# Setup of a two-layer token mixer: modulation weights in four blocks of their own, first groups fed two feature tiles at a time, and two reordered stage ends

## The chip, the cores and the metric

The kernel runs on one core of one Trainium2 chip. The metric is the device time of one execution in microseconds (us), lower is better; the runs given are the median of three. The trace is one profiled execution of the same program.

## The reference, cut to what matters

Two layers of a conditioned mixer (`x` of 512 tokens, `ctx` of 256 tokens, 1024 features), then one block of another kind (not touched here). Per layer:

```python
sh1, sc1, g1, sh2, sc2, g2 = split(silu(c) @ w_mod[l] + b_mod[l], 6)        # and the same for c_ctx
u  = x * (1 + sc1) + sh1;   uc = ctx * (1 + csc1) + csh1
y, yc = token_mixer(u, uc, ...)     # u @ w_in -> convolution, mLSTM and latent attention; gated merge @ w_out
x  = layer_norm(ALPHA * x + g1 * y, ln1_g, ln1_b)
h  = square(relu((x * (1 + sc2) + sh2) @ w1 + b1)) @ w2 + b2
x  = layer_norm(ALPHA * x + g2 * h, ln2_g, ln2_b)
```

Everything is fp32. Products are made from a high and a low part of each operand: high x high, high x low, low x high, so each 128-column group of weights costs three matmuls per feature tile and token range.

## The kernel before, in words

**Weights.** All big weights go through a ring of `SLOTS = 4` slots (`core.ring`), 128 columns x 1024 rows (512 KB) a slot, loaded by SyncE (SP) in the order of `plan_weights`, each when `weights_used` says that its slot is free. A group of weights is then split: ScalarE (ACT) rounds it into one of two high slots (`high_part`, L365), GpSimd (POOL) subtracts (`low_part`, L374). `product` (L448, matmuls at L470, L471, L475) needs the high part from the start and the low part for its last third. `paired_products` (L493, matmuls at L505, L506, L510) runs the first two groups of a stage interleaved, feature tile k by feature tile k, so that features may arrive while it runs. Both take `between` hooks.

**Setup (`setup_stage`).** The first 16 groups of `w_mod` of layer 0 (shift 1 and scale 1, 8 MB) are the first run `mod0` of the ring. SP issues the constants, four ring groups, `x`, `ctx`, then the other twelve groups as slots come free, then the first four groups of `w_in`. TensorE (PE) turns each pair of groups into rows of sums (`mod_rows_pair`, L723), with the transposes of the tokens in between (L681), copied to `core.x` by VectorE (DVE, L702); then it transposes nine tiles of small vectors (L688, each waits for a copy at L705), turns the rows back to columns (`turn_mod_rows`, L732), and DVE adds the bias and the one (`mod_finish`, L740, L745). Only then `Modulated.make_high` (ACT, L830, L836) and `make_low` (DVE, L848, L863) make the features of layer 0 tile by tile, and the first product of the projection starts (`project_stage`, PE L505).

**Attention end (`attention_stage`).** Head pairs p are worked through in steps i over key tiles. The sums of pair p-1 are inverted by DVE during pair p (`invert`, L1846) at the steps of `inverse_at`; POOL then divides (L1777), and `invert_last` (L1856) of the last pair waits for that division, because both use the same tile. Behind it on DVE stands a copy of modulation rows (`copy_mods`, L1866) on which PE's last `turn_mod_rows` (L732) waits.

**MLP head (`out_mlp_stage`, once per layer).** After `w_out` the first layer norm's sums are taken by PE in the middle of the first paired products of `w1` (after tile `SUMS_AFTER` = 4). ACT takes the logarithm and the exponential, DVE refines the root in three instructions (L3282, L3284), and only then evicts group 0: `cols` (L3292, L3293), `pre` from PSUM (L3298), which frees the PSUM tile for the next product. In the same loop DVE normalises the residual (L3304, L3306) and ACT scales it (L3178). In layer 0 tiles are 768 tokens wide, in layer 1 512.

```python
for q in range(KT):
    dve.wait_ge(used.sem, group_done(core, run, i, q))
    ...
    ins = nc.vector.scalar_tensor_tensor(piece(pre), piece(mean), cols[:, j:j + 1], result[j](q % 2), ALU.mult, ALU.add)
    ins.then_inc(free[q % 2].sem, 1)
```

## Time and profile before

| | us |
|---|---|
| median of 3 runs (lowest, highest) | 3375.93 (3370.58, 3377.02) |
| the profiled execution | 3375.39 |
| its span | 3373.6 |
| mean granted TensorE clock | 0.983 |

| engine | busy us | share |
|---|---|---|
| PE (matmul) | 3247.3 | 96% |
| PE weight load | 2600.0 | 77% |
| DVE | 1870.1 | 55% |
| ACT | 1180.1 | 35% |
| POOL | 1093.2 | 32% |

An engine's busy time is the time in which it executes instructions; the waits of an engine are listed with the instruction that released it. "Granted clock" is TensorE's clock as a share of full speed: 1.00 is 2.4 GHz, 0.50 is 1.2 GHz.

### The profile page before, as it was taken

Reading aid. Unit: us, or ns where it says so; the run is one execution under the profiler, and the core shown is the slowest. Engines: PE = TensorE matmul, PEld = TensorE weight load, DVE = VectorE, ACT = ScalarE, POOL = GpSimd, SP = SyncE. Lnnn points to the kernel's source line nnn. Section 1 sums busy time; section 2 is a strip of 40 time slices with the busy share of each in tenths; the row PEclk is TensorE's granted clock in tenths of the full one; section 3 lists DMA queues with packets and bytes.
Section 4 is the critical chain, followed back from the end, with each engine's and each line's share of the span. In section 5 each row is a group of like instructions: output and inputs, shape, how many; then the busy total and the mean of one; then the engine's idle time right before and its main releaser. Section 6 shows DMA issues by size and latency. Waiting matters only on the chain. (4 is left out here: it accounts for less than half of the span.)

```text
span 3373.6 us, 48742 instructions
## 1 busy us (share of the span) xinstructions
PE 3247.3 (96%) x18116; PEld 2600.0 (77%) x18116; DVE 1870.1 (55%) x2848; ACT 1180.1 (35%) x1670; POOL 1093.2 (32%) x551
## 2 busy tenths in 40 slices
PE   5999999999999999999999999999999989999998
PEld 4888655788888888888776457778888867788886
DVE  2869466622368242245997564138333575777634
ACT  2233333631244132233542436234322364323223
POOL 2433100422233322222441014443444424344442
PEclk8999999999999999999999999999999989999999
DMA  6222255022221222222322341332333321233332
GB/s 187 63 61 55 49 155 152 17 60 63 63 63 57 63 63 63 63 63 62 88 75 47 107 119 45 93 94 81 94 93 93 91 74 51 82 93 93 95 96 78
DMA packets 549133, 270.17 MB, mean 80 GB/s; under 512 B 55922, under 2 KB 547146, under 8 KB 548827
## 3 DMA queue, kind: packets, MB, share of 16 engines
q1 hardware_dynamic: 547330, 267.20, 28.0%
q8 instruction: 127, 2.08, 0.3%
q14 instruction: 51, 0.42, 0.0%
q10 hardware_dynamic: 889, 0.30, 0.0%
q0 software_dynamic: 736, 0.17, 0.0%
HBM read 265.50 MB, written 2.10 MB: 79 GB/s over the span
## 5 line engine op out<-in xcount | busy, mean ns | idle before, releaser
L374 POOL TENSOR_TENSOR weights_low<-weight_ring,weights_high 128x1024 fp32r<-128x1024 f32 (+1 forms) x403 | 965.4, 2397 | 1755.3 <-ACT weights_high L365 1754.9
L365 ACT ACTIVATE weights_high<-weight_ring 128x1024 fp32r<-128x1024 f32 (+1 forms) x408 | 410.0, 1005 | 1132.3 <-PE ps L475 1048.7
L470 PE MATMUL ps<-features_high,weights_high 128*128 128x512 f32 (+1 forms) x1888 | 640.1, 354 | 4.7 <-DVE features_low L2476 4.6
L471 PE MATMUL ps<-features_low,weights_high 128*128 128x512 f32 (+1 forms) x1888 | 636.4, 353 | 0.0
L470 PEld LDWEIGHTS ps<-features_high,weights_high 128*128 128x128 f32 x1888 | 356.0, 189 | 64.7 <-DVE features_low L2476 6.5
L471 PEld LDWEIGHTS ps<-features_low,weights_high 128*128 128x128 f32 x1888 | 355.6, 188 | 55.1 <-issue 0.2
L475 PE MATMUL ps<-features_high,weights_low 128*128 128x512 f32 (+1 forms) x1888 | 383.8, 351 | 0.0
L470 PE MATMUL ps<-u_high,weights_high 128*128 128x512 f32 (+2 forms) x944 | 369.3, 394 | 11.5 <-ACT weights_high L365 3.3
L471 PE MATMUL ps<-u_low,weights_high 128*128 128x512 f32 (+2 forms) x944 | 362.8, 388 | 0.0
L475 PEld LDWEIGHTS ps<-features_high,weights_low 128*128 128x128 f32 x1888 | 304.6, 188 | 47.0
L1249 DVE SCALAR_TENSOR_TENSOR conv<-conv,vectors 128x512 f32<-128x512 f32 (+1 forms) x480 | 306.3, 707 | 1.2 <-DVE conv L1157 0.9
L470 PE MATMUL ps<-mlp_u_high,weights_high 128*128 128x512 f32 (+1 forms) x960 | 273.3, 314 | 7.6 <-DVE arena L3298 7.6
L471 PE MATMUL ps<-mlp_u_low,weights_high 128*128 128x512 f32 (+1 forms) x960 | 271.0, 313 | 0.0
L3235 DVE SCALAR_TENSOR_TENSOR x_features<-ps,modulation,x_features 128x512 f32<-128x512 f32 x118 | 74.8, 661 | 314.5 <-PE ps L475 302.9
L475 PE MATMUL ps<-u_high,weights_low 128*128 128x512 f32 (+2 forms) x944 | 227.5, 384 | 0.0
L470 PEld LDWEIGHTS ps<-u_high,weights_high 128*128 128x128 f32 (+1 forms) x944 | 180.2, 191 | 59.0 <-issue 9.6
L2498 DVE TENSOR_TENSOR arena<-ps,arena 128x768 f32<-128x768 f32 (+3 forms) x48 | 39.5, 823 | 329.9 <-PE ps L475 329.6
L471 PEld LDWEIGHTS ps<-u_low,weights_high 128*128 128x128 f32 (+1 forms) x944 | 179.8, 190 | 39.0 <-issue 1.2
L475 PEld LDWEIGHTS ps<-u_high,weights_low 128*128 128x128 f32 (+1 forms) x944 | 170.8, 187 | 38.1 <-issue 0.5
L470 PEld LDWEIGHTS ps<-mlp_u_high,weights_high 128*128 128x128 f32 x960 | 184.0, 192 | 20.8 <-issue 8.1
L471 PEld LDWEIGHTS ps<-mlp_u_low,weights_high 128*128 128x128 f32 x960 | 183.8, 191 | 11.0
L3169 ACT ACTIVATE arena<-arena,seam 128x512 f32<-128x512 f32 x96 | 59.1, 647 | 291.2 <-DVE arena L3301 291.2
(609 smaller groups left out, 4927.5 us busy)
## 6 DMA issues: line engine op xcount, KB each, us to landing
weight_ring<-in_w_in SPq DMA_DIRECT2D x262, 256.0 KB, 3.2
weight_ring<-in_w SPq DMA_DIRECT2D x256, 256.0 KB, 3.0
weight_ring<-in_w_mod SPq DMA_DIRECT2D x192, 256.0 KB, 3.7
weight_ring<-in_w_up SPq DMA_DIRECT2D x88, 256.0 KB, 3.1
weight_ring<-in_w_out SPq DMA_DIRECT2D x48, 256.0 KB, 3.3
weight_ring<-in_w_down SPq DMA_DIRECT2D x32, 256.0 KB, 3.2
weight_ring<-in_w_mla_out SPq DMA_DIRECT2D x32, 128.0 KB, 2.3
weight_ring<-in_w_conv_out SPq DMA_DIRECT2D x32, 128.0 KB, 2.3
```

Source lines behind the costliest of these rows:

```text
L365: act.activation(core.ring_high[:, split_slot(run, q), 0:n], core.ring[:, slot, 0:n], ACT.Copy).then_inc(core.high_ready.sem, 1)
L374: pool.tensor_tensor(core.ring_low[:, split_slot(run, q), 0:n], core.ring[:, (run.first + q) % SLOTS, 0:n], high.bitcast(F32), ALU.subtrac ...
L470: pe.matmul(to, w_high[:, k, 0:m], high(k, a, b), start=(first and k == ks[0]), stop=False, skip_group_check=True)
L471: pe.matmul(to, w_high[:, k, 0:m], low(k, a, b), start=False, stop=False, skip_group_check=True)
L475: mm = pe.matmul(out[:, at:at + b - a], w_low[:, k, 0:m], high(k, a, b), start=False, stop=(last and k == ks[-1]), skip_group_check=True)
L1249: nc.vector.scalar_tensor_tensor(conv[:, f, a:b], pads[:, f, bass.ds(t + at, b - a)], w_dw[:, bass.ds(t, 1), f], conv[:, f, a:b], ALU.mult ...
L2498: nc.vector.tensor_tensor(dst, gemm(core, 2 + f, w), sig[:, f, 0:w], ALU.mult).then_inc(multiplied.sem, 1)
L3169: ins = act.activation(tmp[:, a:b], pre[:, a:b], ACT.Relu, bias=cols[:, ns + j:ns + j + 1])
L3235: ins = nc.vector.scalar_tensor_tensor(x, gemm(core, q % 2)[:, a:b], mod[:, gates + q, j:j + 1], x, ALU.mult, ALU.add)
```

## The change

Four edits. In the setup, the 16 modulation groups leave the ring: `FirstModulation` holds them in four blocks (m = 0 to 3) of 2 MB, two of them in a new allocation `near` and two in the arena, each with shift and scale of feature tiles 2m and 2m+1. SP issues the constants, the tokens in three loads, block 0, two ring groups of `w_in`, the last 18 small vector loads (taken from ACT's queue), blocks 1 to 3, two more ring groups. Only block 0 is turned before the projection; the others are turned by hooks inside the first paired products, and ACT and DVE make the features two tiles at a time. The tokens are transposed one tile of 128 tokens after the other, and the vectors' nine transposes have a PSUM place each and are copied by two instructions. In the projection SP waits until two ring groups are used before it loads `rope` (whose place `near` had) and goes on with the ring.

```diff
-            add(f"mod{l}", MOD_FIRST, plain(w_mod), split=False)
...
+    def make_rows(self, pe, m):
+        pe.wait_ge(self.loaded[m].sem, self.loaded[m].at(32))
+        for kind in range(2):
+            w, to = self.blocks[m][:, :, kind, :], self.in_rows[kind]
+            for half in range(KT // 2):
+                for j in range(COND_TILES):
+                    k, g = 2 * half + j % 2, j // 2
+                    mm = pe.matmul(to[j * COND_ROWS:(j + 1) * COND_ROWS], self.core.cond[:, k, :], w[:, k, g * P:(g + 1) * P],
...
+            mm.then_inc(self.made.sem, 1)
+    def copy_rows(self, act, m):
+        for kind in range(2):
+            act.wait_ge(self.made.sem, self.made.at(2 * m + kind + 1))
+            act.activation(self.rows[:, 2 * m + kind], self.in_rows[kind], ACT.Copy).then_inc(self.copied.sem, 1)
+    def turn_rows(self, pe, m):
+        for n in range(2 * m, 2 * m + 2):
+            pe.wait_ge(self.copied.sem, self.copied.at(n + 1))
+            mm = pe.matmul(self.sums[:, 4 * n:4 * n + 4], self.rows[:, n], self.core.cond_pick, start=True, stop=True)
+        mm.then_inc(self.turned.sem, 1)
+    def finish(self, dve, m):
...
+            if kind:
+                ins = v.scalar_tensor_tensor(mod[:, at:at + 2, :], sums, 1.0, bias, ALU.add, ALU.add)
+            else:
+                ins = v.tensor_tensor(mod[:, at:at + 2, :], sums, bias, ALU.add)
...
     def _(sp):
         sp.dma_start(core.base, a["base"]).then_inc(base_in.sem, 16)
+        for n in range(0, NT, 2):
+            sp.dma_start(tokens[:, n:n + 2], source.rearrange("(n p) c -> p n c", p=P)).then_inc(tokens_in[n // 2].sem, 16)
+        first.load(sp, 0)
+        load_weights(core, sp, LEAD)
+        load_vectors(sp, ACT_SHARE, len(tiles), sp_loaded)
+        for m in range(1, 4):
+            first.load(sp, m)
         load_weights(core, sp, SLOTS)
...
+        sp.wait_ge(used.sem, core.runs[f"conv{l}"].first + (2 if seam is None else 0))
         sp.dma_start(core.rope, core.rope_input).then_inc(core.rope_loaded.sem, 16)
...
+        first_mods = {0: lambda: core.first.make_rows(pe, 1), 1: lambda: turn_and_make(1, 2), 2: lambda: core.first.turn_rows(pe, 2),
+                      3: lambda: core.first.make_rows(pe, 3), 4: lambda: core.first.turn_rows(pe, 3)}
...
@@ project_stage, scalar (ACT) @@
+            for m in range(4):
+                core.u.make_high(act, range(2 * m, 2 * m + 2), lambda k: core.first.wait(act, k // 2))
+                if m < 3:
+                    core.first.copy_rows(act, m + 1)
@@ project_stage, vector (DVE) @@
+            for m in range(4):
+                if m:
+                    core.first.finish(dve, m)
+                core.first.wait(dve, m)
+                core.u.make_low(dve, range(2 * m, 2 * m + 2))
```

In the attention, the inversions during the last pair move to its first steps:

```diff
     inverse_at = {0: [(0, 0)], 2: [(0, 1)], 4: [(1, 0)]} if both else {0: [(0, 0)], 5: [(0, 1)]}
+    inverse_at_last = {0: [(0, 0)], 1: [(0, 1)], 2: [(1, 0)]} if both else {0: [(0, 0)], 1: [(0, 1)]}
...
+            for ctx, which in (inverse_at if p + 1 < PAIRS else inverse_at_last).get(i, []) if p else []:
+                invert(p - 1, ctx, which)
```

In the MLP head, DVE evicts the first two groups before it refines the root (the second into a tile and columns of its own), ACT splits the next two groups of weights between logarithm and exponential and behind it, the residual is normalised in the second half of the first quarter, the sums are taken one tile later in layer 1, and ACT splits the last early group before the squares of a tile:

```diff
+SUMS_AFTER = (4, 5)
@@ scalar (ACT) @@
         for k in range(KT):
             g = k + LEAD
             if g < KT:
                 high_part(core, act, run_out, g // 4, g % 4)
             else:
                 high_part(core, act, run, 0, g - KT)
+            if k == KT - 1:
+                square(made(KT - 2))
...
         act.activation(rstd[:, 0:w], var[:, 0:w], ACT.Ln, bias=core.eps[:, 0:1]).then_inc(s["logged"].sem, 1)
+        ahead(core, act, run, 0, 0, False)
...
+        ahead(core, act, run, 0, 1, False)
...
+                if first_here and q >= 2:
                     ahead(core, act, run, i, q, last)
@@ vector (DVE) @@
+        for q in range(2):
+            evict(0, q)
         step = s["rstd_step"]
...
+                if not (isinstance(i, int) and i == 0 and q < 2):
+                    evict(i, q)
...
-                    nc.vector.tensor_tensor(x, x, mean[:, 0:w], ALU.subtract).then_inc(s["centered"].sem, 1)
-                    nc.vector.tensor_tensor(x, x, rstd[:, 0:w], ALU.mult).then_inc(s["normalised"].sem, 1)
...
+                if first_here:
+                    for n in (0, 1) if q == 0 else range(q + 1, min(q + 2, KT)):
+                        normalise(n)
```

The order of SP's queue in the setup, before:

```order
L645 DMA constants<-in_base 128x900
L308 DMA weight_ring<-in_w_mod 128x4x128 x8
L647 DMA arena<-in_x 128x4x1024
L648 DMA arena<-in_ctx 128x2x1024
...
L308 ISA [waits weights_used_0]
L308 DMA weight_ring<-in_w_mod 128x4x128
```

and with the change:

```order
L717 DMA constants<-in_base 128x900
L720 DMA features<-in_x 128x2x1024 x2
L720 DMA features<-in_ctx 128x2x1024
L608 DMA first_modulation<-in_w_mod 128x8x256 x2
L305 DMA weight_ring<-in_w_in 128x4x128 x4
L695 DMA arena<-in_ffn_conv_w 22x128 [waits rows_cleared_21]
...
L700 DMA arena<-in_c_norm_g 1x64 x2
L608 DMA first_modulation<-in_w_mod 128x8x256 x2
L608 DMA arena<-in_w_mod 128x8x256 x4
L305 DMA weight_ring<-in_w_in 128x4x128 x4
L1030 DMA rope<-in_rope 128x1152 [waits weights_used_0]
```

The tokens stand ahead of all modulation weights, three quarters of these stand behind two ring groups and the small vectors, and no load of the setup waits for a slot any more.

PE from the setup into the first paired products, with the change (before, the eight L732 matmuls all stand ahead of the first L505; L502, L503, L507 are the lines that were L505, L506, L510):

```order
L751 MATMUL ps<-constants,features 128x128 x48
L618 MATMUL ps<-first_modulation,conditions 32x128 x32
L761 MATMUL ps<-constants,arena 128x128 x9
L632 MATMUL ps<-constants,arena 128x4 x2
...
L502 MATMUL ps<-features_high,weights_high 128x256
L503 MATMUL ps<-features_low,weights_high 128x256
L618 MATMUL ps<-first_modulation,conditions 32x128 x32
L502 MATMUL ps<-features_high,weights_high 128x512
...
L632 MATMUL ps<-constants,arena 128x4 x2
L618 MATMUL ps<-arena,conditions 32x128 x32
```

Three of four blocks of the modulation are now made (L618) and turned (L632) between feature tiles of the first pair.

DVE in the MLP head of layer 1, before:

```order
L3277 TENSOR_SCALAR arena<-arena 128x512 [waits at_conv_step_82]
L3282 TENSOR_TENSOR arena<-arena 128x512 [waits at_conv_squared_80,at_conv_step_82]
L3282 TENSOR_TENSOR arena<-arena 128x512 [waits at_conv_squared_80]
L3284 SCALAR_TENSOR_TENSOR arena<-arena 128x512 [waits at_conv_squared_80]
L3292 TENSOR_SCALAR seam1<-ps 128x1 [waits weights_used_0,at_conv_scaled_83,at_conv_squared_80]
L3293 TENSOR_SCALAR seam1<-ps,vectors 128x1
L3298 SCALAR_TENSOR_TENSOR arena<-arena,seam1,ps 128x512 [waits at_conv_centered_79]
L3301 TENSOR_TENSOR arena<-arena 128x512 [waits product_tile0_free_3]
L3304 TENSOR_TENSOR x_features<-x_features,arena 128x512
```

and with the change (L3398 was L3298, L3406 and L3408 were L3282 and L3284, L3422 was L3301):

```order
L3383 TENSOR_SCALAR arena<-arena 128x512 [waits at_conv_step_94]
L3392 TENSOR_SCALAR seam1<-ps 128x1 [waits weights_used_0,at_conv_scaled_95,at_conv_step_94]
L3393 TENSOR_SCALAR seam1<-ps,vectors 128x1
L3398 SCALAR_TENSOR_TENSOR arena<-arena,seam1,ps 128x512 [waits at_conv_centered_91]
L3392 TENSOR_SCALAR seam1<-ps 128x1 [waits weights_used_0]
L3393 TENSOR_SCALAR seam1<-ps,vectors 128x1
L3398 SCALAR_TENSOR_TENSOR arena<-arena,seam1,ps 128x512 [waits at_conv_centered_91]
L3406 TENSOR_TENSOR arena<-arena 128x512 [waits at_conv_squared_92] x2
L3408 SCALAR_TENSOR_TENSOR arena<-arena 128x512 [waits at_conv_squared_92]
L3422 TENSOR_TENSOR arena<-arena 128x512 [waits product_tile0_free_3,at_conv_squared_92]
```

The two evictions stand ahead of the three instructions of the refinement, and L3304, L3306 are no longer among the evictions. (Semaphores carry the name of their first use.)

## Rows read from the trace of the kernel before

**Rows 1.** The page, busy time of each engine, share of the span, instructions.

```profile
PE 3247.3 (96%) x18116; PEld 2600.0 (77%) x18116; DVE 1870.1 (55%) x2848; ACT 1180.1 (35%) x1670; POOL 1093.2 (32%) x551
```

**Rows 2.** Waits of PE, whole span (total us, times, longest us).

```profile
PE ps L723 <- DMA weight_ring<-in_w_mod: 16.3, 6, 3.8
...
PE ps L505 <- DVE features_low L863: 12.3, 4, 4.7
...
PE ps L470 <- DVE arena L3298: 7.6, 2, 4.1
```

**Rows 3.** Timeline of the setup: SP's queue and PE (start us, us, what).

```profile
0.75 0.40 SPq L645 DMA_DIRECT2D constants<-in_base  x1
...
1.20 6.12 SPq L308 DMA_DIRECT2D weight_ring<-in_w_mod  x8
...
8.58 0.85 SPq L648 DMA_DIRECT2D arena<-in_ctx  x1
...
23.66 2.82 PE L681 MATMUL ps<-constants,arena 128*128 128x128 f32 x12 [7.14 <-DMA arena<-in_ctx]
...
28.37 1.08 PE L723 MATMUL ps<-weight_ring,conditions 128*32 128x128 f32 x32 [1.89 <-DMA weight_ring<-in_w_mod]
```

**Rows 4.** DMA issues, 0 to 60 us (KB each, median us to landing).

```profile
constants<-in_base SPq DMA_DIRECT2D x1, 450.0 KB, 3.7
```

**Rows 5.** Two setup stretches: length, PE, PEld, DVE, ACT, POOL busy; PEclk, DMA, GB/s.

```profile
15.00:20.00 5.00, 1.52 (x31) 1.06 (x20) 0.00 (x0) 0.00 (x0) 0.00 (x0) 1.00 1.05 371
...
40.00:45.00 5.00, 4.74 (x67) 3.74 (x56) 1.91 (x2) 0.00 (x0) 0.00 (x0) 0.66 0.98 284
```

**Rows 6.** Timeline, end of the setup and first paired products.

```profile
54.32 0.69 PE L688 MATMUL ps<-constants,arena 128*128 128x128 f32 x2 [0.17 <-DVE vectors L705]
...
61.61 0.17 DVE L745 TENSOR_SCALAR modulation<-modulation 128x16 f32<-128x16 f32 x1
...
64.48 0.76 PE L505 MATMUL ps<-features_high,weights_high 128*128 128x512 f32 x1 [3.14 <-DVE features_low L863]
...
79.91 2.94 PE L510 MATMUL ps<-features_high,weights_low 128*128 128x512 f32 x16
...
82.93 0.47 PE L470 MATMUL ps<-features_high,weights_high 128*128 128x512 f32 x1
```

**Rows 7.** Timeline, MLP head of layer 0, PE and DVE.

```profile
1045.24 2.98 PE L510 MATMUL ps<-mlp_u_high,weights_low 128*128 128x512 f32 x16
...
1051.71 0.77 PE L470 MATMUL ps<-mlp_u_high,weights_high 128*128 128x512 f32 x1 [3.49 <-DVE arena L3298]
...
1050.42 1.14 DVE L3298 SCALAR_TENSOR_TENSOR arena<-arena,seam,ps 128x512 f32<-128x512 f32 x2
```

**Rows 8.** Timeline, MLP head of layer 1, PE, DVE and POOL.

```profile
2321.86 0.38 PE L505 MATMUL ps<-mlp_u_high,weights_high 128*128 128x256 f32 x1 [2.42 <-ACT weights_high L365]
...
2338.64 0.55 PE L470 MATMUL ps<-mlp_u_high,weights_high 128*128 128x256 f32 x1 [4.09 <-DVE arena L3298]
...
2346.83 0.28 PE L470 MATMUL ps<-mlp_u_high,weights_high 128*128 128x256 f32 x1
...
2334.68 2.71 DVE L3284 SCALAR_TENSOR_TENSOR arena<-arena 128x512 f32<-128x512 f32 x1
...
2334.43 2.41 POOL L374 TENSOR_TENSOR weights_low<-weight_ring,weights_high 128x1024 fp32r<-128x1024 f32 x1 [9.99 <-ACT weights_high L365]
```

**Rows 9.** Stretches at either clock level, columns as in rows 5.

```profile
1051.00:1054.00 3.00, 2.29 (x7) 1.94 (x8) 2.93 (x5) 1.38 (x3) 0.00 (x0) 0.50 0.12 35
...
1057.00:1060.00 3.00, 3.00 (x18) 2.65 (x18) 2.97 (x4) 0.00 (x0) 2.21 (x1) 0.96 0.00 0
...
2347.00:2350.00 3.00, 3.00 (x27) 3.00 (x27) 2.90 (x7) 0.80 (x2) 0.00 (x0) 1.00 0.55 162
```

**Rows 10.** Timeline, attention end of layer 1, DVE and PE.

```profile
2000.65 1.76 DVE L1856 RECIPROCAL conv<-ps 128x256 f32<-128x256 f32 x1 [1.45 <-POOL features L1777]
...
2002.61 0.49 PE L732 MATMUL ps<-constants,conv 128*128 128x4 f32 x2 [2.38 <-DVE conv L1866]
```

More of the change, by code:

```diff
@@ L658, in _ @@
         act.activation(core.cond[:, :, 0:2], cond_turn.rearrange("p (j k) -> p k j", k=KT), ACT.Silu).then_inc(cond_ready.sem, 1)
-        load_vectors(act, SHARE, len(tiles), loaded)
-        act.wait_ge(core.weights_used.sem, run.first + run.groups)
-        act.activation(mod_rows[:, half:], in_rows[:, half:], ACT.Copy).then_inc(rows_copied.sem, 1)
+        load_vectors(act, POOL_SHARE, ACT_SHARE, act_loaded)
+        first.copy_rows(act, 0)
         first_high_parts(core, act, core.runs["conv0"])
@@ L683, in _ @@
-        pe.wait_ge(pool_loaded.sem, 16 * n_vec(0, SHARE))
-        pe.wait_ge(loaded.sem, 16 * n_vec(SHARE, len(tiles)))
+        for n in range(NT):
+            pe.wait_ge(tokens_in[n // 2].sem, 16)
+            if n >= 2:
+                pe.wait_ge(token_copied.sem, 2 * (n - 1))
+            for f in range(KT):
+                mm = pe.transpose(turn_of(n)[:, f * P:(f + 1) * P], tokens[:, n, f * P:(f + 1) * P], core.ident)
+            mm.then_inc(turned.sem, 1)
+        pe.wait_ge(cond_ready.sem, 1)
@@ L690, in _ @@
-        pe.wait_ge(turn_free.sem, 2 + KT + len(tiles))
-        pe.wait_ge(rows_copied.sem, 2)
-        turn_mod_rows(core, pe, lambda pair: mod_rows[:, pair * P:(pair + 1) * P], MOD_FIRST // 2, sums).then_inc(rows_turned.sem, 1)
+            mm = pe.transpose(vector_turn(n), rows[:, n, :], core.ident)
+        mm.then_inc(vectors_turned.sem, 1)
+        first.turn_rows(pe, 0)
     @block.vector
     def _(dve):
-        dve.sem_inc(turn_free.sem, 2)
-        for f in range(4):
+        for f in range(2, 4):
@@ L699, in _ @@
             dve.sem_inc(core.tile_free[f].sem, 1)
-        for f in range(KT):
-            dve.wait_ge(turned.sem, f + 1)
-            nc.vector.tensor_copy(core.x[:, f, :], psum(f)).then_inc(turn_free.sem, 1)
-        for n in range(len(tiles)):
-            dve.wait_ge(turned.sem, KT + n + 1)
-            nc.vector.tensor_copy(core.vec[:, n * P:(n + 1) * P], psum(n)[:, 0:P]).then_inc(turn_free.sem, 1)
-        dve.wait_ge(core.weights_used.sem, run.first + run.groups)
-        nc.vector.tensor_copy(mod_rows[:, 0:half], in_rows[:, 0:half]).then_inc(rows_copied.sem, 1)
@@ L1278, in project_stage @@
         core.u.passed()
+        core.first.passed()
     else:
@@ L3007 @@
 SEAM = 64
-SUMS_AFTER = 4
+SUMS_AFTER = (4, 5)
 def out_mlp_stage(core, l, seam):
```

213 lines of the change are left out of this document (131 added, 82 removed).

## The prediction

> **What bounds the kernel now.** I read the page first. TensorE is busy for 96% of the span and no other engine for more than 55% [rows 1], so time is to be had only where PE stands still or runs at the lower clock level. The second view is therefore PE's own waits [rows 2]. They show three things that the change touches: 16.3 us for modulation weights in the setup, 12.3 us for the low parts of features, and 7.6 us in two waits for an eviction, one at each MLP head. A fourth, 2.38 us, is at the attention end of layer 1 [rows 10]. The third is the timeline at each place. In the setup SP issues constants and eight ring loads before the tokens, and PE gets the last of these, `ctx`, at 23.66 [rows 3]. All bytes issued up to it are 450 + 8 x 256 + 2048 + 1024 = 5570 KB, or 5.70 MB, and they took 23.66 - 0.75 = 22.9 us: 249 GB/s. The DMA engines are full both in a stretch with the tokens (371 GB/s) and in one with ring loads alone (284 GB/s) [rows 5]. Twelve further groups of modulation weights follow through the ring, the vectors are still being turned at 54.32, and the first product of the projection starts at 64.48, ends its pair at about 82.9 [rows 6]. What counts is when that pair ends: from there PE is never short of work for long.
>
> The sum is made against the profiled execution, 3375.39 us, which is 0.5 us below the median of 3375.93. About 0.2% (7 us) is what a measurement of this kernel can tell from no change.
>
> **The setup, step by step.** *Start of the first product.* SP now issues constants, tokens, block 0 and two groups of `w_in` (the two DMA groups together 3.15 MB), in all 450 + 3072 + 2048 + 1024 = 6594 KB, or 6.75 MB, and then 18 small loads of vectors; the nine transposes of the vectors need all of it. At the 249 GB/s of before it has landed at 0.75 + 27.1 = 27.9; at 284 to 371 GB/s at 19 to 24.5. The early stretch starts slowly, but the block's rows are 1 KB long where the ring's are 512 bytes, so I take 26. Then nine transposes at 0.69 / 2 us [rows 6] are 3.1 us, two copies of 1152 columns together 1.7 (768 took 1.14 [rows 7]), two matmuls and two DVE instructions (0.17 each [rows 6]) for block 0 0.5, and from ready modulation to first product 64.48 - 61.78 = 2.7 us as before [rows 6]. 26 + 3.1 + 1.7 + 0.5 + 2.7 = 34.0, with 28 and 37 as ends.
>
> *The pair.* Its eight feature tiles took 79.91 - 64.48 = 15.4 us, 1.93 each, and the 16 low products that end it 3.0 [rows 6]. To them come three times 32 small matmuls (1.08 us where they ran fastest [rows 3]) and three times two turning ones (0.4): 4.5 us. From each turning PE cannot go on to the next two feature tiles until DVE has finished the block (0.4) and the features are made (2.7): 3.1 us, in part under the matmuls of the next block or of the second tile. I get about 2.0, 1.7 and 1.4 us of standing still for the blocks 1, 2 and 3. The last block is landed 6.29 MB after 26, at 43 to 51; PE asks for it at about 47. So the pair ends at 34.0 + 15.4 + 4.5 + 5.1 + 3.0 = 62.0. These gaps pull the clock down at times: the same 3 us held 7 matmuls in 2.29 us at 0.50 and 27 at 1.00 in another stage [rows 9]; I add 2. **64 instead of 82.9, 19 us less.** The ends are 69.5 (249 GB/s throughout, lower level) and 59.
>
> On the queues: POOL's four vector tiles instead of three and ACT's three are issued while the tokens move; on SP the wait for two used groups holds back `rope` and ring group 4, and behind them every later weight. It ends with the pair, and two further groups, already in the ring, give PE 16 us (48 matmuls each at 6 per us [rows 9]) for one `rope` and one group, some 1.1 MB: hidden. DVE's and ACT's later work in the stage moves with PE.
>
> *Where a rule of the notes applies.* The clock was 0.66 from 40 to 45 us, in a setup full of breaks [rows 5], and 0.50 after a wait of 3.49 us [rows 7, 9]: PE's breaks decide the level. The Trainium skill, "TensorE: Matmul & The Clock Gate", Part 1 (the HAM clock gate), says that "the default state is throttled, and activity releases the throttle", which speaks against cutting the first pair into pieces with waits between them. By it the whole pair would run at the lower level, which is a rival below; the trace agrees with it at the places named and says nothing on breaks as short as those expected here.
>
> **MLP head, layer 0.** The pair ends at 1048.2, the next product starts at 1051.71 because its tile is freed by DVE's eviction at 1050.42 [rows 7]. With the eviction ahead of the refinement, DVE has group 0 out while the second group's 16 low products run, and the high part needed is split earlier too. The 3.5 us go. The lower level that follows lasts until about 1057 (0.96 is the mean from there on [rows 9]), 5.3 us at 7 / 2.29 = 3.1 matmuls per us against 18 / 3 = 6: 2.6 us, which go with the wait. 6 us. Behind it, DVE refines and handles groups 0 and 1 and reaches the eviction of group 2 at about 1065, when PE needs that tile (two groups of 48 matmuls after 1048.2, at 6 per us): nothing to spare, so the lower end is 3.
>
> **MLP head, layer 1.** PE first waits 2.42 us for ACT's high part, which stands behind two squares [rows 8]; it now stands ahead of one of them: 2.1 us less. The wait of 4.09 us for the eviction goes. The group that follows ran from 2338.64 to 2346.83 [rows 8], 8.2 us, at the lower level, against 48 x 3.00 / 27 = 5.3 at the upper [rows 9]: 2.7. That is 8.9. What is late next: DVE evicts group 2 only behind the refinement and the finishing of groups 0 and 1, at about 2344.2, 0.5 later than PE wants it, and POOL's subtraction may stretch one instruction of it, as L3284 took 2.71 us beside a POOL instruction of 2.41 us [rows 8]. I take 1.4 for both: **7.5**, ends 5 and 9. The Trainium skill, "SBUF — State Buffer", "SBUF: two separate sides", has the port pair of DVE and GpSimd as an exclusive lock, in which the loser waits for the whole instruction; by it the stretch falls onto whichever DVE instruction POOL meets, and the trace agrees with 2.71 us. The residual's normalising, two DVE instructions and one or two of ACT per tile, moves into the second half, where DVE has one addition per product: hidden.
>
> **Attention ends.** In layer 1 DVE waits 1.45 us for POOL's division before its last inversions, and PE then 2.38 us for a copy behind them [rows 10]. With the inversion done five steps earlier the division is long over: 1.6 us less, up to 4 if the lower level that follows goes too, 0 at least. In layer 0 no such wait is seen: 0.
>
> **Sum.** 19 + 6 + 7.5 + 1.6 = 34.1; 3375.4 - 34.1 = 3341.3, and 0.5 for the median: **3342 us**.
>
> **Rivals.**
> - *The lower level through the whole pair.* Breaks of 1 to 2 us between short bursts hold PE at 0.50. For: 0.50 to 0.66 in the setup [rows 5]. Against: after the wait of 2.42 us [rows 8] PE went on at the upper level. The pair's 18.4 + 4.5 us become up to 1.9 times as long, of which the waits take back 5, and 2 were already counted: about 10 us more, 3352.
> - *The heads give it back.* DVE is late for group 2 in both layers, because the refinement now comes behind two evictions and under a POOL subtraction: 2 and 3 us stay of 6 and 7.5. 3342 + 8.5 = 3350.
> - *The blocks land together.* Everything is in the queue within some 20 us; if the loads share the engines rather than follow each other, block 0 and the vectors land late, at about 35, and the pair ends at 72: 3350. For: the 249 GB/s up to 23.66 us is less than either stretch shows, as if later loads had taken a part. Against: `ctx`, the last of eleven loads, still came at 23.66 [rows 3].
> - *Better than that.* 340 GB/s, no lower level in the pair, clean heads, the clock at the attention end: 23 + 7 + 9 + 3.5 = 42.5, 3333.
> - *Slower than before.* The 18 small loads on SP's queue take their turn one behind the other. At the 3.7 us from issue to landing of the constants [rows 4], with 18 in a row, the vectors would be complete at 26 + 67 = 93, and the pair would end near 131: 48 us later than before, 15 given back elsewhere, 3409. It decides from 34 / 18 = 1.9 us each. Against: eight ring loads and two large ones, issued by 9.4, had all landed by 23.66 [rows 3], so loads of one queue run beside each other.
> - *It does nothing where it says.* If DMA bandwidth alone sets the pair's end, 13.2 MB at 249 GB/s is 53.8, and it cannot come before 60: still 3342. There is no room for no change at all in the setup.
>
> **How the numbers follow.** Forecast 0.50; lower level 0.17; heads 0.12; blocks together 0.07; better 0.10; slower 0.02; the rest, a mishap that eats all but the bound, 0.02. The forecast's own range is 3336 to 3348. The range to hold 8 in 10 takes in most of the two rivals above and the better case: 3333 to 3356. All but the last two are faster by over 0.2%: 0.96; within 0.2% 0.02, slower 0.02.
>
> **What would show it.** Right: first product of the projection at 31 to 37 us and the next product after the pair at 60 to 68; DVE's evictions ahead of the refinement with PE going from the pair into group 2 with no wait in either layer; no wait over 1 us before group 4; POOL's division before the last inversions. Wrong: the vectors' transposes later than 30, PE waits for w_mod of over 3 us inside the pair, a granted clock near 0.5 from 34 to 60, or a new wait of PE for L3398 at group 4.

## The result, and the profile after

The median of the changed kernel is 3346.81 us (3343.38 to 3351.27, 5 runs) against 3375.93 (3370.58 to 3377.59, 5 runs): a ratio of 0.9917, 95% interval 0.9905 to 0.9928, or 29.1 us less. 34 were forecast. A second measurement of the same kernel (`changed_again`, below) gave 23.9 us less. The profiled execution took 3347.69 us, 27.7 less than the one before; the ledger below is made against that.

The page, its head, the busy line and the line of the clock:

```profile
span 3345.8 us, 48674 instructions
...
PE 3238.5 (97%) x18116; PEld 2594.1 (78%) x18116; DVE 1905.9 (57%) x2850; ACT 1183.5 (35%) x1677; POOL 1092.4 (33%) x552
...
PEclk8999999999999999999999999999999999999999
```

PE is busy for 8.8 us less than in [rows 1], though it has the same products to make. The mean granted clock rose from 0.983 to 0.986, which by proportion (an estimate) is some 10 us of 3247, so the lower busy time fits the clock; the rest of the gain is waits. PE's waits, longest in total first (engine, line waited for, us in total, times, longest):

```profile
PE ps L502 <- DVE features_low L939: 16.1, 6, 4.7
...
PE ps L618 <- DMA first_modulation<-in_w_mod: 4.5, 1, 4.5
PE ps L467 <- DVE features_low L3427: 3.7, 2, 3.4
```

Of the waits of [rows 2], 16.3 us for modulation weights (L723) became 4.5 (L618), and the 7.6 for evictions are gone but for 0.9. The wait for low parts of features (L505, now L502) rose from 12.3 to 16.1, and one is new: 3.7 us, of which 3.4 in one piece, for `hidden_low` (L3427).

SP's queue in the setup (start, time to issue), for [rows 3]:

```profile
2.69 6.89 SPq L608 DMA_DIRECT2D first_modulation<-in_w_mod  x2
9.62 10.34 SPq L305 DMA_DIRECT2D weight_ring<-in_w_in  x4
20.00 1.94 SPq L695 DMA_DIRECT2D arena<-in_ffn_conv_w  x3
...
26.95 1.02 SPq L608 DMA_DIRECT2D first_modulation<-in_w_mod  x2
```

From 20.00 to 26.91 SP issued the small loads. They are 19, three of `ffn_conv_w` and sixteen behind them, where the texts on record count 18.

PE in the setup and the pair, for [rows 3] and [rows 6]:

```profile
21.36 3.64 PE L618 MATMUL ps<-first_modulation,conditions 128*32 128x128 f32 x64 [4.46 <-DMA first_modulation<-in_w_mod]
28.20 2.15 PE L761 MATMUL ps<-constants,arena 128*128 128x128 f32 x9 [3.20 <-DMA arena<-in_c_norm_g]
...
35.07 0.76 PE L502 MATMUL ps<-features_high,weights_high 128*128 128x512 f32 x1 [4.06 <-DVE features_low L939]
...
38.53 3.04 PE L618 MATMUL ps<-first_modulation,conditions 128*32 128x128 f32 x64
...
43.79 1.96 PE L618 MATMUL ps<-arena,conditions 128*32 128x128 f32 x64
46.59 0.50 PE L502 MATMUL ps<-features_high,weights_high 128*128 128x512 f32 x1 [0.84 <-DVE features_low L939]
...
58.96 0.50 PE L502 MATMUL ps<-features_high,weights_high 128*128 128x512 f32 x1 [2.01 <-DVE features_low L939]
...
62.56 2.94 PE L507 MATMUL ps<-features_high,weights_low 128*128 128x512 f32 x16
65.59 0.47 PE L467 MATMUL ps<-features_high,weights_high 128*128 128x512 f32 x1
```

The vectors were complete at 28.20, the first product started at 35.07, and the next product after the pair at 65.59 where it was 82.93 [rows 6].

Layer 0's head, for [rows 7]: from the pair into group 2 without a wait.

```profile
1025.81 2.98 PE L507 MATMUL ps<-mlp_u_high,weights_low 128*128 128x512 f32 x16
1028.62 0.39 PE L467 MATMUL ps<-mlp_u_high,weights_high 128*128 128x512 f32 x1
```

Layer 1's head, PE, for [rows 8]: the product of group 2 at 2303.39 needs no wait, group 4 waits 0.86 us, and the end of w2's first product 3.41.

```profile
2290.88 0.36 PE L502 MATMUL ps<-mlp_u_high,weights_high 128*128 128x256 f32 x1 [1.55 <-DVE x_features L3341]
...
2303.39 0.28 PE L467 MATMUL ps<-mlp_u_high,weights_high 128*128 128x256 f32 x1
...
2315.77 0.36 PE L467 MATMUL ps<-mlp_u_high,weights_high 128*128 128x256 f32 x1 [0.86 <-DVE arena L3398]
...
2347.07 0.50 PE L467 MATMUL ps<-features_high,weights_high 128*128 128x512 f32 x1 [3.41 <-DVE features_low L3427]
```

The same place, DVE's work for group 2 and POOL's subtraction beside it:

```profile
2306.11 2.77 DVE L3408 SCALAR_TENSOR_TENSOR arena<-arena 128x512 f32<-128x512 f32 x1
...
2314.88 0.75 DVE L3398 SCALAR_TENSOR_TENSOR arena<-arena,seam,ps 128x512 f32<-128x512 f32 x1
2315.66 2.15 DVE L3422 TENSOR_TENSOR arena<-arena 128x512 f32<-128x512 f32 x1
2318.60 0.69 DVE L3424 TENSOR_TENSOR arena<-arena 128x512 f32<-128x512 f32 x1 [0.79 <-ACT arena L3277]
2319.34 0.69 DVE L3427 TENSOR_TENSOR features_low<-arena,features_high 128x512 fp32r<-128x512 f32 x1
```

```profile
2305.59 2.74 POOL L371 TENSOR_TENSOR weights_low<-weight_ring,weights_high 128x1024 fp32r<-128x1024 f32 x1 [0.78 <-ACT weights_high L362]
2314.88 2.38 POOL L371 TENSOR_TENSOR weights_low<-weight_ring,weights_high 128x1024 fp32r<-128x1024 f32 x1 [6.56 <-ACT weights_high L362]
```

L3398, with an operand in PSUM, takes 0.75 us beside POOL's L371. L3422, a multiply of two tiles in SBUF that takes 0.69 alone (the first one at 2308.91 does), takes 2.15. It is so in each of the six groups 2 to 7. The attention end of layer 1, for [rows 10]:

```profile
1974.39 0.39 PE L808 MATMUL ps<-constants,conv 128*128 128x4 f32 x2 [0.68 <-DVE conv L1955]
1974.71 1.08 PE L799 MATMUL ps<-weight_ring,conditions 128*32 128x128 f32 x32
```

**The ledger.** The start of the same PE instruction in both traces, the earlier start in the changed kernel being the gain so far: after the pair 17.3 us; before layer 0's head 19.4; behind it 25.1; ahead of the attention end of layer 1 26.5 and behind it 30.1; in layer 1's head 31.0 at the first wait, 35.3 at group 2, 37.8 at group 3, 36.8 at group 4, 36.7 at the start of w2 and 31.4 at its second product; at the end 27.8. So the setup gave 17.3, layer 0's head 5.7, the attention end 3.6, and layer 1's head 1.3: it gained 6.6 and gave 5.3 back. Stretches of unchanged work between them added 2.1 and 1.4 us and took 3.6 in the last block.

### The profile page after: what moved, and what is told of

Its sections match the earlier page's. It is cut to its first block and busy times, and to the rows that moved or that the text cites. A ratio compares the mean times of both kernels' runs of the same rounds, so it can differ in the third digit from the quotient of the medians.

```text
span 3345.8 us, 48674 instructions
## 1 busy us (share of the span) xinstructions
PE 3238.5 (97%) x18116; PEld 2594.1 (78%) x18116; DVE 1905.9 (57%) x2850; ACT 1183.5 (35%) x1677; POOL 1092.4 (33%) x552
## 5 line engine op out<-in xcount | busy, mean ns | idle before, releaser
L371 POOL TENSOR_TENSOR weights_low<-weight_ring,weights_high 128x1024 fp32r<-128x1024 f32 (+1 forms) x403 | 963.7, 2393 | 1732.3 <-ACT weights_high L362 1732.1
L3341 DVE SCALAR_TENSOR_TENSOR x_features<-ps,modulation,x_features 128x512 f32<-128x512 f32 x118 | 74.9, 662 | 266.7 <-PE ps L472 255.1
```

The costliest lines, as they stand in the source:

```text
L371: pool.tensor_tensor(core.ring_low[:, split_slot(run, q), 0:n], core.ring[:, (run.first + q) % SLOTS, 0:n], high.bitcast(F32), ALU.subtrac ...
L3341: ins = nc.vector.scalar_tensor_tensor(x, gemm(core, q % 2)[:, a:b], mod[:, gates + q, j:j + 1], x, ALU.mult, ALU.add)
```

## The experiments

Lines are named in the text as in the changed kernel; in the rows of a run they are its own. Where the whole times are too coarse, a stretch of the trace decides. "The head's stretch" is that from the norm sums of layer 1's head to the sums at the layer's end: 2327.22 to 2696.44 in the kernel before, 369.2 us, and 2297.38 to 2665.00 in the changed one, 367.6. The changed kernel takes the sums one feature tile later, so these two do not hold the same work: counted from the same matmul, it has 368.8 against 369.2. Among the kernels with the later sums the stretch is the same work, but it varies by itself: `setup_better` and `head_only`, whose head is that of the changed kernel, have 368.8 us where that has 367.6, because the lower clock level behind the wait of 3.4 us lasted longer. A difference of under 1.2 us in it tells nothing.

### The three parts alone

`setup_only` is the kernel before with the setup's part of the diff, of which one line stands for all:

```diff
-        if l == 0:
-            add(f"mod{l}", MOD_FIRST, plain(w_mod), split=False)
```

> The kernel before with the edit of the setup alone. If the parts of the change add up, the next product after the first pair starts at 65.6 us as in the changed kernel (82.9 before), and the whole gain is 17 to 19 us: 3357 to 3359 us. The rival is that the setup's gain is coupled to the rest through clock and phase, so that alone it gives less than 15 or more than 21 us.

3357.67 us against 3376.22, ratio 0.9943 (0.9927 to 0.996): 18.6 us less, and the low products that end the pair start at 62.30, as in the changed kernel (62.56).

`head_only`, the MLP head's part:

```diff
-SUMS_AFTER = 4
+SUMS_AFTER = (4, 5)
...
+        for q in range(2):
+            evict(0, q)
         step = s["rstd_step"]
```

> The kernel before with the edits of the MLP head alone. In the changed kernel's trace layer 0 gained 5.7 us and layer 1 gained 6.6 us up to the first product of w2 and lost 5.2 us again behind it. If this giving back belongs to the head itself, it is here too: a wait of PE of about 3.4 us for hidden_low in layer 1, and 3368 to 3370 us in all. If it came from phases that the other edits shift, that wait is absent and the time is 3363 to 3365 us.

3368.45 us, ratio 0.9974 (0.9964 to 0.9984): 7.8 less. The give-back belongs to the head itself:

```profile
2341.32 0.36 PE L470 MATMUL ps<-mlp_u_high,weights_high 128*128 128x256 f32 x1 [0.86 <-DVE arena L3310]
...
2372.60 0.80 PE L470 MATMUL ps<-features_high,weights_high 128*128 128x512 f32 x1 [3.39 <-DVE features_low L3339]
```

`attention_only`:

```diff
+    inverse_at_last = {0: [(0, 0)], 1: [(0, 1)], 2: [(1, 0)]} if both else {0: [(0, 0)], 1: [(0, 1)]}
...
-            if p and i in inverse_at:
-                for ctx, which in inverse_at[i]:
-                    invert(p - 1, ctx, which)
+            for ctx, which in (inverse_at if p + 1 < PAIRS else inverse_at_last).get(i, []) if p else []:
+                invert(p - 1, ctx, which)
```

> The kernel before with the earlier inversions alone. By the prediction 1.6 us are gained at the end of attention in layer 1; by the changed kernel's trace 3.7 us, as the lower clock level behind the wait of 2.38 us goes as well. So 3372 to 3374 us, within what the measurement can tell from nothing; the place itself decides: PE's turning matmul after the second set of modulation rows no more waits 2.38 us, and the modulation matmuls behind it take 1.1 us and not 1.94.

3371.25 us, ratio 0.9985 (0.9975 to 0.9995). At the place, the wait of 2.38 us is 0.68, and the stretch around it (from the first product of keys at 1892.03 in the kernel before to the mLSTM's first eight-matmul transposes at 2020.11) takes 124.5 us instead of 128.1. `setup_only`, without the edit, has 128.1 there, but `head_only`, also without it, 126.5: up to 1.6 of the 3.6 us can be the clock. The three medians add up to 31.3 us, against 29.1 for all together: as far as medians of this spread can tell, the parts do not lean on each other.

### Why layer 1's head gave its gain back

`normalise_in_loop`: the residual's normalising in layer 1 back where it was.

```diff
                 nc.vector.tensor_tensor(made_here, made_here, rstd[:, 0:w], ALU.mult).then_inc(s["evicted"].sem, 1)
+                if not both and isinstance(i, int) and i == 0:
+                    normalise(q)
...
-                if first_here:
+                if first_here and both:
                     for n in (0, 1) if q == 0 else range(q + 1, min(q + 2, KT)):
                         normalise(n)
```

(and ACT's `residual(q)` with it).

> The changed kernel, but in layer 1 the residual is normalised inside the first quarter's loop again, as before. Theory A, POOL's subtraction stretches DVE's multiply by the root in every group (0.69 to 2.16 us), and DVE, at 5.39 us a group against PE's 5.68, never catches up: with 1.30 us more work per group, of which 0.79 fill a wait, a group costs 5.9 us, DVE falls further behind, and PE's wait for hidden_low before the end of w2's first product grows from 3.4 to some 5 to 7.5 us: 3349 to 3351 us. Theory B, moving the normalising out of the loop is what made DVE late: the wait goes, as in the kernel before, and the time is 3341 to 3343 us.

```profile
2322.21 0.36 PE L467 MATMUL ps<-mlp_u_high,weights_high 128*128 128x256 f32 x1 [1.74 <-DVE arena L3400]
...
2351.84 0.50 PE L467 MATMUL ps<-features_high,weights_high 128*128 128x512 f32 x1 [0.67 <-DVE features_low L3431]
...
2357.93 0.79 PE L467 MATMUL ps<-features_high,weights_high 128*128 128x512 f32 x1 [5.13 <-DVE features_low L3431]
```

3357.82 us, ratio 0.9947 (0.993 to 0.9964); the head's stretch took 374.1, 6.4 more than in the changed kernel. The waits grew to 0.67 and 5.13, 5.8 together, within the 5 to 7.5 of theory A; the whole missed its 3349 to 3351 by 7 us, of which 3.2 stand in the clock's stretch (42.7 us for 39.4, see `changed_again`). Theory B falls: moving the normalising out was worth 6.4 us to this order of the work.

`quarter_low`: POOL's subtraction over a quarter of the columns. Three quarters of the low parts of the weights of layer 1's MLP are left out.

```diff
-    n = run.kts[q] * P
+    n = run.kts[q] * P // (4 if run is core.runs["mlp1"] else 1)
     high = core.ring_high[:, split_slot(run, q), 0:n]
```

> The changed kernel, with POOL's subtraction for the weights of layer 1's MLP over a quarter of the columns (three quarters of those low parts are left out, so that POOL's instruction takes about 0.6 us and not 2.4). Theory A: DVE's multiply takes 0.7 us again, a group 3.9 us, DVE catches up within three groups, and PE's wait of 3.4 us for hidden_low goes with the lower clock level behind it, as does the 0.86 us wait at group 4: 3341 to 3342 us. Theory C, DVE is late because the refinement now stands behind two evictions: less than 2.1 us of the 3.4 go, 3344 to 3346 us.

DVE in groups 2 and 3 of this run:

```profile
2305.09 1.11 DVE L3408 SCALAR_TENSOR_TENSOR arena<-arena 128x512 f32<-128x512 f32 x1
...
2312.20 0.75 DVE L3398 SCALAR_TENSOR_TENSOR arena<-arena,seam,ps 128x512 f32<-128x512 f32 x1
2312.98 0.69 DVE L3422 TENSOR_TENSOR arena<-arena 128x512 f32<-128x512 f32 x1
...
2316.12 0.75 DVE L3398 SCALAR_TENSOR_TENSOR arena<-arena,seam,ps 128x512 f32<-128x512 f32 x1
2316.90 0.69 DVE L3422 TENSOR_TENSOR arena<-arena 128x512 f32<-128x512 f32 x1
```

L3422 takes 0.69 us in each group, a group 3.9 and not 5.4, the refinement (L3408) 1.11 and not 2.77. PE has no wait of over 0.6 us from group 2 to the end of w2's first product, and the head's stretch is 361.3 us, 6.3 less. The whole was 3345.3 us (ratio 0.9913, 0.9896 to 0.993), not the 3341 to 3342 of theory A and inside the 3344 to 3346 of theory C; but its four runs span 3340.8 to 3346.8, so it decides nothing. The rows decide: with POOL's instruction short both waits are gone, and nothing of the refinement's place behind two evictions is left over. Theory A stands, and theory C falls.

`last_tile_last`: w2's first two products in another order.

```diff
+                held = i == 0 and not both
+                if held:
+                    for q, ks in ((0, range(0, 7)), (1, range(0, 5)), (0, range(7, 8)), (1, range(5, 8))):
+                        product(core, pe, run, i, KT + q, use(i, KT + q), q % 2, *hidden, width=w, first=ks[0] == 0, last=ks[-1] == 7,
+                                late=1 if len(ks) == 7 else 0, ready=None if q else hidden_ready, ks=ks, done=ks[-1] == 7)
-                for q in range(KT):
+                for q in range(2 if held else 0, KT):
```

> The changed kernel, with the first two products of w2 in layer 1's first quarter taken in another order: tiles 0 to 6 for the first, 0 to 4 for the second, then tile 7 for the first and 5 to 7 for the second. Tile 7 is then wanted 3.5 us later, when it was ready. If the give-back is this wait of 3.4 us and 1.6 us of lower level behind it, 5 us go: 3341 to 3343 us. If DVE is simply behind with everything, the wait moves on to the third product, which needs its tile freed by DVE behind two normalisings: 3344 to 3346 us.

```profile
2356.30 0.50 PE L467 MATMUL ps<-features_high,weights_high 128*128 128x512 f32 x1 [1.33 <-ACT weights_high L362]
```

The wait of 3.41 is gone, and PE waits 1.33 for ACT's high part at the third product instead. The stretch is 364.2 us, 3.4 less. The whole, 3348.96 us (ratio 0.9922, 0.9905 to 0.9938), missed the 3341 to 3343 expected, and by more than those 1.3 us: other stretches were longer (see the clock, below).

### The setup

`vectors_on_act`:

```diff
-POOL_SHARE, ACT_SHARE = 4, 7
+POOL_SHARE, ACT_SHARE = 4, 9
```

> The changed kernel, with the 18 small vector loads back on ACT's queue, where loads were issued at 0.3 us each and ended at 14.6 us. SP's own issuing was held up for 10.3 us by four ring loads, so it came to the small loads at 20.0 and the vectors were complete at 28.2. Theory D, the issuing on SP bounds the vectors: they are complete at 23 to 25, the first product starts at 31 to 32 (35.07), the blocks 1 to 3 are issued 7 us earlier, and the pair ends at 59 to 62: 3341 to 3343 us. Theory E, the bytes bound them (249 GB/s up to 28.2): the vectors still come at 27 or later and the time stays at 3345 to 3348 us.

```profile
20.28 0.60 ACTq L700 DMA_DIRECT2D arena<-in_c_norm_g  x2
...
21.82 3.64 PE L618 MATMUL ps<-first_modulation,conditions 128*32 128x128 f32 x64 [5.56 <-DMA first_modulation<-in_w_mod]
25.44 1.31 PE L762 MATMUL ps<-constants,arena 128*128 128x128 f32 x9
...
33.90 0.77 PE L502 MATMUL ps<-features_high,weights_high 128*128 128x512 f32 x1 [6.81 <-DVE features_low L940]
```

The features, in the changed kernel and then in this run:

```profile
32.40 1.65 DVE L924 TENSOR_SCALAR arena<-x_features,modulation 128x512 f32<-128x512 f32 x4
```

```profile
28.80 4.09 DVE L925 TENSOR_SCALAR arena<-x_features,modulation 128x512 f32<-128x512 f32 x4
32.81 1.81 DVE L940 TENSOR_TENSOR features_low<-arena,features_high 128x768 fp32r<-128x768 f32 x2
```

```profile
26.83 4.83 POOL L371 TENSOR_TENSOR weights_low<-weight_ring,weights_high 128x1024 fp32r<-128x1024 f32 x2 [11.80 <-ACT weights_high L362]
```

The vectors no longer bound anything: their transposes follow block 0's rows at 25.44 with no wait. So it was SP's queue and not the bytes: theory E falls. But the modulation was ready 3.6 us earlier and the first product only 1.2: POOL's two subtractions, which in the changed kernel ended at 31.0, ahead of DVE's features at 32.40, now ran beside them, and L924's four instructions took 4.09 us and not 1.65. 3347.73 us, ratio 0.9917 (0.9901 to 0.9934): the expectation of 3341 to 3343 was wrong. In the setup it was so by the same mechanism as in the head, and the pair ended at 64.30, not at 59 to 62. The whole time alone lies in theory E's 3345 to 3348, but the clock's stretch (see `changed_again`) was 3.2 us longer here than in the changed kernel's trace, so the rows decide here too.

### Better versions

`setup_better` adds two edits to `vectors_on_act`, POOL's second subtraction behind the first two feature tiles and block 3's rows one hook earlier, behind feature tile 2 and not 3 (the text below says two):

```diff
-        first_low_parts(core, pool, core.runs["conv0"])
+        low_part(core, pool, core.runs["conv0"], 0, 0)
...
+        if seam is None:
+            core.u.wait(pool, 1)
+            low_part(core, pool, runs["conv"], 0, 1)
         low_parts(core, pool, runs["conv"], made=LEAD)
...
-        first_mods = {..., 2: lambda: core.first.turn_rows(pe, 2),
-                      3: lambda: core.first.make_rows(pe, 3), 4: lambda: core.first.turn_rows(pe, 3)}
+        first_mods = {..., 2: lambda: turn_and_make(2, 3),
+                      3: lambda: core.first.turn_rows(pe, 3)}
```

> The changed kernel with three edits of its setup: the small loads on ACT's queue (as in the run vectors_on_act), POOL's second subtraction of weights put behind the first two feature tiles (there the two subtractions, 4.8 us in one piece, stretched DVE's four feature instructions from 1.65 to 4.09 us), and block 3's rows made two tiles earlier. If POOL took the gain of the earlier vectors, the first product starts at 31 to 32 us (33.9 in vectors_on_act, 35.1 in the changed kernel); with rows 3 earlier PE's wait of 2.01 us before tile 6 goes too, and the next product after the pair starts at 59.5 to 61.5 (64.3 and 65.6): 3342 us, with 2 to 3 us to either side for clock phases elsewhere. If blocks 2 and 3 land too late for the faster pair, PE waits for them at the rows of block 3 and the pair ends at 62 or later.

3343.53 us, ratio 0.9904 (0.9889 to 0.9919). The first product came at 31.22, PE waited once in the pair (0.84 us), the wait of 2.01 is gone, and the next product started at 58.63 (65.59 in the changed kernel, 59.5 to 61.5 expected).

`head_better` is `last_tile_last` with ACT's `ahead` in front of two `residual` calls and with

```diff
+                early = not both and isinstance(i, int) and i == 0
+                if early and q == 1:
+                    evict(0, 2)
```

> The changed kernel with three edits of layer 1's MLP head: tile 7 wanted last (as in last_tile_last), ACT splitting the third product's weights ahead of two residual instructions (they cost PE 1.33 us there), and DVE evicting group 2 before it finishes group 1. In the place itself the waits of 0.86, 3.41 and 1.33 us are gone and the head ends 5.5 to 6 us earlier than in the changed kernel against the work ahead of it: 3341 us, again with 2 to 3 us to either side. If DVE's lag only moves on, a wait of PE for a freed tile of 1 us or more stands at w2's third or fourth product.

3348.93 us, ratio 0.9917 (0.9902 to 0.9932), and the stretch 364.9, where `last_tile_last` had 364.2: no gain, and a difference too small to call a loss. Group 2 evicted earlier moved the wait on: PE stood 0.93 us for ACT's high part at group 4 and 1.19 us for DVE at group 5. A miss.

> The six edits of setup_better and head_better together. If they add up, 10 to 11 us less than the changed kernel: 3336 us (3333 to 3340), a ratio to the kernel before of 0.988.

`both_better`: 3342.83 us (3334.69 to 3343.63), ratio 0.9895 (0.9881 to 0.9909). Slower than the 3336 expected, in part for the miss above. Without the early eviction:

> The kernel of both_better without the early eviction of group 2, which only moved the wait: there PE waited 0.93 us for ACT's high part and 1.19 us for DVE at the groups behind. The stretch from the first layer norm sums of layer 1's head to the end of that layer, 367.6 us in the changed kernel, 364.2 with tile 7 last and 364.9 in both_better, becomes 362.9 (3.4 and 1.3 us less than 367.6), the next product after the first pair starts at 59 to 60 us, and the whole is 6 + 4.7 us less than the changed kernel: 3336 us, 3333 to 3341 as the clock falls elsewhere. If ACT's order at tile 7 is worth nothing, the stretch is 364.2.

```profile
31.93 0.76 PE L502 MATMUL ps<-features_high,weights_high 128*128 128x512 f32 x1 [4.82 <-DVE features_low L940]
...
59.33 0.47 PE L467 MATMUL ps<-features_high,weights_high 128*128 128x512 f32 x1
...
2348.97 0.47 PE L467 MATMUL ps<-features_high,weights_high 128*128 128x512 f32 x1 [0.74 <-DVE x_features L3354]
```

`five_edits`: 3342.03 us (3332.62 to 3344.33), ratio 0.9899 (0.9882 to 0.9916). The pair ends 6.3 us earlier than in the changed kernel; the head's stretch is 363.7 (362.9 expected), as 0.74 us of waiting for a tile took the place of the 1.33 for the high part. Against `setup_better` (3343.53) the whole time does not tell the head's two edits from nothing; they are seen in the stretch alone.

> The changed kernel itself once more, beside five_edits on the same chip. 3346.8 us (3343 to 3351). Its stretches of identical work elsewhere tell how far the clock alone moves the time: in the traces so far the stretch from the gates' small transposes to the keys of layer 1 took 39.4 to 42.7 us, the same work in every kernel. If that is chance and no property of a program, it may be near 42 us here, where it was 39.4.

`changed_again`, the changed kernel itself, measured beside `five_edits`: 3351.60 us (3350.49 to 3351.79), ratio 0.9931 (0.9918 to 0.9945). `five_edits` is 9.6 us faster beside it, and the ranges and intervals do not meet: it beats both kernels. The clock is not the reason, as its stretch described next took 42.6 us in `five_edits` and 42.4 in `changed_again`. The changed kernel had 3346.81 in its first measurement, outside the range of the second. The clock is where the two traces part. The stretch from the gates' small transposes to the keys in layer 1, the same work everywhere, took 39.4 us there and 42.4 here; 20 us in it, windows of the changed kernel and of `changed_again` (PE, weight load, DVE, ACT, POOL busy; granted clock; DMA share; GB/s):

```profile
1760.00:1780.00 20.00, 18.44 (x118) 16.30 (x119) 19.90 (x40) 5.08 (x12) 5.11 (x2) 0.91 0.23 48
```

```profile
1760.00:1780.00 20.00, 18.03 (x100) 16.21 (x101) 19.90 (x43) 4.43 (x7) 3.24 (x2) 0.74 0.14 32
```

In the traces of this study that stretch has three values: 41.2 us in the three kernels without the edit of the MLP head (the kernel before, `setup_only`, `attention_only`), and with it 39.4 to 39.7 in four traces and 42.4 to 42.7 in seven. The changed kernel is in both of the last two groups, so no edit decides between them; what does was not tried.

## Why the prediction was right, and where not

**The setup: 19 us forecast, 17.3 measured.** The first product was due at 34.0 and came at 35.07. The step "I take 26" for the landing was wrong in kind. Block 0 had landed at 21.36 (277 GB/s for its 5.70 MB, within the bounds taken), and what came at 28.20 were the small loads, because SP got to issue them only at 20.00, after four ring loads had held it for 10.34 us. I had priced bytes and read no issue times; `vectors_on_act` shows it. Behind that the terms hold: from ready modulation to the first product 2.7 us as before, nine transposes with copies and block 0 some 4.2 where 5.3 were taken.

**The pair** was to take 28.0 + 2 and took 30.5, by luck: two errors cancel. "Three times 32 small matmuls" is the step that failed: a block is two pairs of groups, 64 matmuls in the trace (the program's 32 are recorded as two each, as the 32 of [rows 3] for one pair are), 3.0 us at the lower level and 1.96 at the upper, 7.0 in all where 3.2 were counted. Against it the gaps were 0.84 and 2.01 us, not 5.1: DVE and ACT made the features mostly under the next block's rows. The clock was 0.51 from 20 to 40 us and 0.98 from 40 to 60, so the rival of the lower level through the pair did not come. (Its own sum was off as well: 22.9 us at up to 1.9 times, less 5 and 2, are 13.6 us more and not 10.) The rule of the Trainium skill quoted for it ("TensorE: Matmul & The Clock Gate", Part 1), that throttled is the default and activity releases it, agrees with the trace as it stands: the lower level held through the first feature tile and into block 1's rows. That the whole pair would stay there did not follow: PE stood still for 0.84 and 2.01 us and went on at the upper level, 1.00 from 42 to 59 us. Nor did block 0 wait for others, nor the small loads queue one behind the other: three were issued in 0.65 us each, the others in 0.25 to 0.31.

**Layer 0's head: 6 forecast, 5.7 measured,** and steady: the stretch from its norm sums to layer 1's first waiting product is 549.9 us before and 544.2 in each of the ten traces of the changed kernel and of those built on it.

**Layer 1's head: 7.5 forecast, 1.3 measured.** The terms that were priced came: 0.9 of 2.1 for the high part (DVE's L3341 is late next there), 4.3 of 4.1 for the eviction, 2.5 of 2.7 for the level (8.2 less 5.3 is 2.9, a slip of 0.2), and 1.1 of 1.4 lost at group 4. The step that failed is "I take 1.4 for both": I followed DVE's lag to the first tile that PE wants back, and stopped. At group 2 DVE was late by one product. To catch up it needs groups shorter than PE's 5.68 us; with POOL's subtraction locked onto L3422 in every group it has 5.39, and regains 0.3 a group. So tile 7's `hidden_low` was ready at 2347.0 where PE wanted it at 2343.7, which cost 3.4 us and, at the lower level that followed, 1.7 more. `normalise_in_loop`, `quarter_low` and `last_tile_last` show the chain from both sides. The lock could have been read in the kernel before:

```profile
2342.89 2.46 DVE L3301 TENSOR_TENSOR arena<-arena 128x512 f32<-128x512 f32 x1
```

There the overlap passed: the same instruction took 0.69, 1.35, 1.13, 0.92 and 0.71 us in groups 2 to 6, as DVE kept to PE's 5.68 us a group and POOL's subtractions came every 5.46. In layer 0 L3422 is stretched too (2.92 us for 0.96), but a group of PE takes 8.5 us there and nothing waits. The rival "the heads give it back" named this cause, DVE behind under a POOL subtraction, for the wrong place and both layers. It left 5 us to the two heads, which gave 7.0, where the forecast had 13.5; its sum, 3350, lies nearer to both measurements than the forecast's 3342.

The rule of the Trainium skill on the shared port pair ("SBUF — State Buffer", "SBUF: two separate sides") says more than I used of it: it names for the lock a DVE instruction with two inputs in SBUF (against a GpSimd instruction that reads SBUF), or one in a mode that uses both ports. The rows agree: L3422 2.15 and L3408 2.77 us (0.69 and 1.11 in `quarter_low`) have two inputs in SBUF; L3398, whose second tile is in PSUM, takes 0.75 either way. L924, with one tile as input, took 4.09 us for four and not 1.65; in which mode it runs, no trace here shows.

**The attention end: 1.6 forecast, 3.6 in the trace**, inside the ends of 0 and 4. PE's matmuls behind the wait ran at the upper level, 1.08 us for a set and not 1.94. As up to 1.6 of the 3.6 can be the clock (`head_only`, above), the edit's own share is between 2.0 and 3.6 us.

Sum: 34.1 forecast, 27.9 measured by these four terms. The range and the sign held since four fifths of the gain lay in two terms that were well sized. Part of it is luck: stretches of unchanged work gave 3.5 us and took 3.6. In its second measurement the kernel took 3351.6 us, inside the wide range of 3333 to 3356 but outside the forecast's own 3336 to 3348. Of the signs named beforehand, one of those for "wrong" came, a new wait of PE for L3398 at group 4, of 0.86 us, and "no wait over 1 us before group 4" failed by the 1.55 us at layer 1's first paired product.

## What to carry to other kernels

When a wait is removed, follow the lag of the engine that caused it to the end of the loop, not to the next wait: compare its period per group, with everything that stretches it, with the period of the engine it feeds. Where POOL works in step with DVE, look which DVE instruction it falls on, every time round. And price a load by when its queue can issue it, before pricing its bytes: small loads that gate a stage go on a queue with nothing large ahead of them.

## What the runs showed of the hardware

- SP took longer to issue a load when much had been issued just before it. Two token loads of 1 MB at the start took 0.94 us together; the two loads of 1 MB of block 0 behind them took 6.89, and four ring loads of 256 KB behind those 10.34, where eight such took 6.12 us at the start before [rows 3]. After 7 us of small loads two more of 1 MB took 1.02. ACT's queue meanwhile issued small loads at 0.3 us each. Whether bytes, rows or the number of loads set this was not tried.
- A multiply of two SBUF tiles was held to POOL's end plus 0.55 us (2317.26, 2317.81), and so in each of six groups: POOL's subtraction started within 0.01 us of L3398 every time, in one rhythm of 5.39 us. With POOL's instruction cut to a quarter the next groups took DVE's own 3.9 us.
- The median of one program moved by 4.8 us between two measurements; the five runs of the first span 7.9 us, those of the second 1.3. Differences of a few us were told only by the stretches of the trace in which the edit lies, and even there identical work varied, by 1.2 us in the head's stretch and by 3 us in the clock's.
